# Routing groups and gathered rows spread together over six tiles of 14 up blocks, with one route buffer, a row ring of its own and one of the two one-hots on ScalarE

## The reference

```python
    s1, i1 = lax.top_k(s[:, :, 0], PEER_TOPK)
    s2, i2 = lax.top_k(s[:, :, 1], PEER_TOPK)
    ...
    w = jax.nn.softmax(top_s, axis=-1)
    ...
        a = jnp.einsum('td,thkd->thk', hb, u[ib], preferred_element_type=jnp.float32)
        coef = (wb * jax.nn.gelu(a, approximate=False)).astype(v.dtype)
        return jnp.einsum('thk,thkd->td', coef, v[ib])
```

## Time and profile before

| | us |
|---|---|
| median of 3 runs | 4797.13 |
| lowest, highest | 4784.73, 4804.99 |
| profiled execution, its own time | 4789.41 |
| profiled execution, span of the core | 4787.7 |
| TensorE busy | 4331.5 (90%) |
| VectorE busy | 2986.1 (62%) |
| ScalarE busy | 1384.7 (29%) |
| GpSimd busy | 1407.8 (29%) |
| mean granted TensorE clock | 0.951 of 2.4 GHz |

### The profile page before, as it was taken

How to read it: one execution, slowest core, us unless ns; L and a number is a source line. 1 busy time by engine, 2 the same in 40 slices (tenths; PEclk the granted TensorE clock), 3 DMA queues, 4 the chain that set the end, 5 groups by cost and what they waited for, 6 DMA issues and landing times.

```text
span 4787.7 us, 58551 instructions
## 1 busy us (share of the span) xinstructions
PE 4331.5 (90%) x21163; PEld 3663.4 (77%) x21163; DVE 2986.1 (62%) x3412; ACT 1384.7 (29%) x1485; POOL 1407.8 (29%) x643
## 2 busy tenths in 40 slices
PE   7899998999988998689999998899997899999997
PEld 2587777777766876577999997889986788777776
DVE  1334656445534652554799997677775677777777
ACT  0323232333332121132333444222222233322322
POOL 0002333000001320122566443677761233233330
PEclk9899999999989999889999999899998999999998
DMA  8325665000013664266555568999996899888885
GB/s 287 100 79 156 186 186 160 31 31 26 20 36 114 190 175 113 70 149 149 123 144 143 136 173 204 346 367 360 355 367 244 346 341 345 329 324 333 332 328 182
DMA packets 716549, 967.22 MB, mean 202 GB/s; under 512 B 137467, under 2 KB 535859, under 8 KB 680371
## 3 DMA queue, kind: packets, MB, share of 16 engines
q1 hardware_dynamic: 638531, 613.29, 41.9%
q0 software_dynamic: 40928, 285.23, 15.6%
q10 hardware_dynamic: 37008, 67.65, 4.9%
HBM read 896.84 MB, written 69.22 MB: 202 GB/s over the span
## 4 chain that ended last, share of the span: by engine, by line
PE 45%; DMA 21%; DVE 19%; issue 7%; ACT 4%; SPq 2%; POOL 1%; DVEq 1%; ACTq 0%; POOLq 0%
PE ps L115 14%; PE ps L116 13%; PE ps L117 13%; DMA gel<-gelu_scratch 11%; DMA pu<-in_peer_u_dram 7%; DVE acc L1761 3%; DVE oneJ L1716 3%; DVE vDl L1434 3%; DVE pT L1623 2%; DMA wm<-in_w_mod_dram 2%; PE ps L1881 1%; DVE mred L1314 1%; DVE ring L1738 1%; PE ps L2039 1%; ACT wh L804 1%
## 5 line engine op out<-in xcount | busy, mean ns | idle before, releaser
L728 POOL TENSOR_TENSOR pTul<-pT,pTuh 128x1024 fp32r<-128x1024 f32 x256 | 650.6, 2542 | 500.3 <-ACT pTuh L1082 498.2
L115 PE MATMUL ps<-h2h,pTuh 128*128 128x384 f32 x2048 | 708.4, 346 | 87.0 <-POOL pTul L728 86.0
L115 PE MATMUL ps<-vDh,coh 128*128 128x512 f32 x1536 | 615.1, 400 | 93.9 <-DVE col L1434 93.3
L117 PE MATMUL ps<-h2h,pTul 128*128 128x384 f32 x2048 | 695.5, 340 | 0.0
L116 PE MATMUL ps<-h2l,pTuh 128*128 128x384 f32 x2048 | 695.3, 339 | 0.0
L116 PE MATMUL ps<-vDl,coh 128*128 128x512 f32 x1536 | 609.6, 397 | 0.0
L117 PE MATMUL ps<-vDh,col 128*128 128x512 f32 x1536 | 608.1, 396 | 0.0
L704 POOL TENSOR_TENSOR mbuf<-mbuf,silu 128x2048 f32<-128x2048 f32 x64 | 255.6, 3994 | 1008.8 <-DMA mbuf<-in_w_mod_dram 1008.0
L742 POOL DMA_INDIRECT ring<-in_peer_v_dram,sidx x128 | 325.5, 2543 | 765.2 <-DVE acc L1761 743.3
L1082 ACT ACTIVATE pTuh<-pT 128x1024 fp32r<-128x1024 f32 x256 | 271.9, 1062 | 835.5 <-DVE pT L1623 824.3
L115 PEld LDWEIGHTS ps<-h2h,pTuh 128*128 128x128 f32 x2048 | 393.0, 192 | 98.4 <-POOL pTul L728 84.4
(11 more groups left out here) (328 smaller groups left out, 8046.0 us busy)
## 6 DMA issues: line engine op xcount, KB each, us to landing
vraw<-in_peer_v_dram SPq DMA_DIRECT2D x128, 1024.0 KB
mbuf<-in_w_mod_dram SPq DMA_DIRECT2D x64, 1024.0 KB, 6.0
pu<-in_peer_u_dram ACTq DMA_DIRECT2D x256, 256.0 KB
pu<-in_peer_u_dram SPq DMA_DIRECT2D x256, 256.0 KB
wraw<-in_w_in_dram SPq DMA_DIRECT2D x48, 1024.0 KB, 8.5
wt<-route_scratch SPq DMA_DIRECT2D x128, 384.0 KB
gel<-gelu_scratch SPq DMA_DIRECT2D x128, 384.0 KB
wm<-in_w_mod_dram SPq DMA_DIRECT2D x16, 2048.0 KB, 8.6
```

Source lines behind the costliest of these rows:

```text
L115: pe.matmul(out, lh, rh, start=first, stop=False)
L117: return pe.matmul(out, ll, rh, start=False, stop=last)
L728: pool.tensor_tensor(pTul[s][:, c, :], pT[s][:, c, :], pTuh[s][:, c, :].bitcast(fp32), ALU.subtract).then_inc(u_lo, 1)
```

## The change

The 84 blocks from 40 to 123 are cut into six tiles of 14 blocks (PT, NT). Each tile makes the route table of 64 tokens, 16 groups, and gathers 20 rows of U. TILE_GROUPS and TILE_ROWS tell how many groups and rows each of its blocks carries: groups in blocks 0 to 10 of the tile, one and two in turn, none in the last three. Blocks 124 to 127 carry two rows each.

- There is one route buffer. Its four parts are stored in the last blocks of the tile, parts 1 and 3 by ScalarE in blocks 11 and 12 and parts 0 and 2 by SyncE in blocks 12 and 13; ScalarE waits for them (`r_stored`) in the next tile's first block.
- The ring for U lies at 168, 176, 184 and 192 KB and no longer shares bytes with the route buffer. For V its fourth buffer is at 56 KB (`ring_v`), so GpSimd waits for the last route stores before it gathers V.
- oneJ is made by ScalarE (`one_j`): absd = |second key - iota| with four Abs activations, then Relu(weight - weight x absd) with four Relu activations, which is the weight where the key matches and 0 elsewhere. `nchw` holds the negative weights; VectorE writes it, with one more instruction in each of three top-k rounds. oneI stays on VectorE (`one_i`).
- GpSimd's first gather waits for the last top-k (`tk_chosen`) instead of the route stores. Its loop over blocks 40 to 65 is now written out.
- On SyncE the first loads of V, route table and gelu come after the last up load instead of after block 67's.

```diff
-RI = 4
 GROUPS = TD // 4
-P1 = GROUPS // RI
-LATE = P0 + P1
+PT = 14
+TILE_GROUPS = (1, 2, 1, 2, 1, 2, 1, 2, 1, 2, 1, 0, 0, 0)
+TILE_ROWS = (2, 1, 2, 2, 2, 1, 2, 2, 2, 1, 2, 0, 0, 1)
...
+RT = 64
+NT = TD // RT
+LATE = P0 + NT * PT
...
+        absd = sb("absd", 200, [P, 4, P])
+        nchw = sb("nchw", 94, [P, TD])
         oneJ = [sb(f"oneJ{s}", 40 + 2 * s, [P, 4, P]) for s in range(2)]
         oneI = [sb(f"oneI{s}", 44 + 2 * s, [P, 4, P]) for s in range(2)]
-        RT = 64
-        route = [sb(f"route{s}", (168, 48)[s], [P, NK, RT]) for s in range(2)]
+        route = sb("route", 48, [P, NK, RT])
...
-        ring = [sb(f"ring{k}", (168, 176, 184, 56)[k], [P, D]) for k in range(4)]
+        ring = [sb(f"ring{k}", (168, 176, 184, 192)[k], [P, D]) for k in range(4)]
+        ring_v = ring[0:3] + [sb("ring_v3", 56, [P, D])]
...
-        def rows_before(i):
-            n = max(0, i - LATE - 2)
-            return min(3 * n, 2 * n + 4)
+        def groups_at(i):
+            r, k = divmod(i - P0, PT)
+            g = 16 * r + sum(TILE_GROUPS[:k])
+            return range(g, g + TILE_GROUPS[k]) if P0 <= i < LATE else range(0)
+        def rows_at(i):
+            r, k = divmod(i - P0, PT)
+            if i < P0:
+                return range(0)
+            if i >= LATE:
+                return range(SLOTS - 2 * (NK - i), SLOTS - 2 * (NK - i) + 2)
+            n = sum(TILE_ROWS) * r + sum(TILE_ROWS[:k])
+            return range(n, n + TILE_ROWS[k])
...
+            def route_store(r, k):
+                sp.wait_ge(r_set, 16 * r + 16)
                 i = slice(32 * k, 32 * k + 32)
-                sp.dma_start(route_d[:, i, bass.ds(4 * (n - 16), RT)], route[s][:, i, :]).then_inc(r_stored[s], 16)
+                sp.dma_start(route_d[:, i, bass.ds(RT * r, RT)], route[:, i, :]).then_inc(r_stored, 16)
...
+            with sp.Fori(0, NT) as r:
+                for k in range(PT):
+                    pre_load(PT * r + P0 + k + 2, k % 2)
+                    if k in (12, 13):
+                        route_store(r, 2 * (k - 12))
+                    pre_store(PT * r + P0 + k - 1, (k - 1) % 2)
...
+            for i in range(LATE, NK - 2):
+                pre_load(i + 2, i % 2)
+                pre_store(i - 1, (i - 1) % 2)
+            sp.wait_ge(r_stored, 64 * NT + 16)
+            sp.wait_ge(r_done, GROUPS)
             for s in range(2):
                 sp.wait_ge(g_stored[s], 16 * 2 + 16)
-            sp.wait_ge(r_done, GROUPS)
             v_load(0, 0, 0)
...
-            with pool.Fori(0, LATE // 2 + 1) as i:
+            with pool.Fori(0, P0 // 2) as i:
                 for s in range(2):
                     for h in range(2):
                         u_low(2 * i + s, s, h)
-            pool.wait_ge(tk_chosen, 2)
-            for ss in r_stored:
-                pool.wait_ge(ss, 64 * (TD // RT // 2) + 16)
-            for i in range(LATE + 2, NK):
-                for k in range(rows_before(i), rows_before(i) + 1):
-                    gather_u(k)
+            for i in range(P0, NK):
                 u_low(i, i % 2, 0)
-                for k in range(rows_before(i) + 1, rows_before(i + 1)):
+                if i == P0:
+                    pool.wait_ge(tk_chosen, DB + 2)
+                for k in rows_at(i):
                     gather_u(k)
                 u_low(i, i % 2, 1)
+            pool.wait_ge(r_stored, 64 * NT + 16)
             for k in range(SLOTS):
...
+            def one_j(g, s):
+                if not isinstance(g, int) or g >= 2:
+                    act.wait_ge(r_done, g - 1)
+                if not isinstance(g, int) or g >= 1:
+                    act.wait_ge(oneJ_set, g)
+                for t in range(4):
+                    ins = act.activation(absd[:, t, :], iota[:, :], ACT.Abs, bias=chT[:, 1, bass.ds(4 * g + t, 1)], scale=-1.0)
+                ins.then_inc(oneJ_abs, 1)
+                act.wait_ge(oneJ_abs, g + 1)
+                for t in range(4):
+                    at = bass.ds(4 * g + t, 1)
+                    ins = act.activation(oneJ[s][:, t, :], absd[:, t, :], ACT.Relu, bias=chT[:, 2, at], scale=nchw[:, at])
+                ins.then_inc(oneJ_set, 1)
+            def keep_route(g, q):
                 act.wait_ge(r_done, g + 1)
-                act.activation(route[slot][:, :, 4 * q:4 * q + 4].rearrange("p i t -> p t i"),
-                               pb[k][:, :].rearrange("p (t i) -> p t i", t=4), ACT.Copy).then_inc(r_set, 1)
-            def route_part(r):
-                for k in range(8):
-                    slot, i, s = k // 4, 8 * r + P0 + k, k % 2
-                    if k % 4 == 0:
-                        act.wait_ge(r_stored[slot], 64 * r + 16)
+                act.activation(route[:, :, 4 * q:4 * q + 4].rearrange("p i t -> p t i"),
+                               pb[6 + q % 2][:, :].rearrange("p (t i) -> p t i", t=4), ACT.Copy).then_inc(r_set, 1)
...
+            def route_tile(r):
+                q = 0
+                for k in range(PT):
+                    i, s, n = PT * r + P0 + k, k % 2, TILE_GROUPS[k]
                     pre_hi(i + 1, 1 - s, 1)
                     pre_load(i + 3, 1 - s)
-                    for q in range(RI):
-                        if q == 2:
-                            pre_hi(i + 2, s, 0)
-                        if q == 3:
-                            pre_gelu(i, s)
-                        keep_route(32 * r + 4 * k + q, 6 + q % 2, slot, 4 * (k % 4) + q)
-            with act.Fori(0, TD // RT // 2) as r:
-                route_part(r)
-            with act.Fori(LATE // 2, NK // 2 - 2) as i:
-                for s in range(2):
-                    up_block(2 * i + s, s)
+                    if k in (11, 12):
+                        route_store(r, 2 * (k - 11) + 1)
+                    for w in range(q, q + n):
+                        one_j(16 * r + w, w % 2)
+                    pre_hi(i + 2, s, 0)
+                    if k == 0:
+                        act.wait_ge(r_stored, 64 * r + 16)
+                    if n == 2:
+                        keep_route(16 * r + q, q)
+                    pre_gelu(i, s)
+                    if n:
+                        keep_route(16 * r + q + n - 1, q + n - 1)
+                    q += n
...
-            def one_hots(g, s):
-                if not isinstance(g, int) or g >= 2:
+                dve.tensor_copy(chT[:, :, bass.ts(b, P)], pb[7][:, 0:3 * P].rearrange("p (w t) -> p w t", w=3))
+                dve.tensor_scalar(nchw[:, bass.ts(b, P)], pb[7][:, 2 * P:3 * P], -1.0, None, ALU.mult).then_inc(ch_set, 1)
+            def one_i(g):
+                if g >= 2:
                     dve.wait_ge(r_done, g - 1)
-                for t in range(4):
-                    at = bass.ds(4 * g + t, 1)
-                    dve.tensor_scalar(oneJ[s][:, t, :], iota[:, :], chT[:, 1, at], chT[:, 2, at], ALU.is_equal, ALU.mult)
-                dve.tensor_tensor(oneI[s][:, :, :], iota[:, :].unsqueeze(1).to_broadcast([P, 4, P]),
-                                  chT[:, 0, bass.ds(4 * g, 4)].unsqueeze(2).to_broadcast([P, 4, P]),
-                                  ALU.is_equal).then_inc(one_set, 1)
-            def route_block(i, s, g):
-                one_hots(g, 0)
-                one_hots(g + 1, 1)
-                u_turn(i + 1, 1 - s, 1)
-                one_hots(g + 2, 0)
-                one_hots(g + 3, 1)
-                u_turn(i + 2, s, 0)
-            route_block(P0, 0, 0)
-            route_block(P0 + 1, 1, 4)
-            with dve.Fori(1, P1 // 2) as r:
-                for s in range(2):
-                    route_block(2 * r + P0 + s, s, 8 * r + 4 * s)
+                dve.tensor_tensor(oneI[g % 2][:, :, :], iota[:, :].unsqueeze(1).to_broadcast([P, 4, P]),
+                                  chT[:, 0, 4 * g:4 * g + 4].unsqueeze(2).to_broadcast([P, 4, P]),
+                                  ALU.is_equal).then_inc(oneI_set, 1)
...
-            for i in range(LATE, NK):
+            dve.wait_ge(ch_set, DB)
+            for i in range(P0, NK):
+                groups, rows = groups_at(i), rows_at(i)
+                for g in groups[0:1]:
+                    one_i(g)
                 if i + 1 < NK:
                     u_turn(i + 1, (i + 1) % 2, 1)
-                for k in range(rows_before(i), min(rows_before(i) + 1, rows_before(i + 1))):
+                for k in rows[0:1]:
                     dot(k)
+                for g in groups[1:2]:
+                    one_i(g)
                 if i + 2 < NK:
                     u_turn(i + 2, i % 2, 0)
-                for k in range(rows_before(i) + 1, rows_before(i + 1)):
+                for k in rows[1:2]:
...
+            def route_tile(r):
+                w = 0
+                for k in range(PT):
+                    for q in range(4):
+                        pre_quarter(PT * r + P0 + k, k % 2, q)
+                        if (q == 3 and TILE_GROUPS[k]) or (q == 1 and TILE_GROUPS[k] == 2):
+                            routing(16 * r + w, w % 2)
```

(1 more changed line is left out.)

75 lines of the change are left out of this document (21 added, 54 removed).

## The result

The changed kernel is **slower** by 0.7%: 4826.7 us, the median of 4 runs (4821.4 to 4832.4), against 4795.7 us, the median of 4 runs of the kernel before on the same chip. The ratio is 1.0066 [1.0041, 1.009]: 31 us more, where 57 less were forecast.

What follows compares the result with a forecast made beforehand. Three limits in turn: VectorE, the handover, then DMA with two gathered rows a block. 835 + 27 + 12 + 3 + 3 = 880 us in place of 937, 57 less: 4797.1 - 57 = 4740 us, range 4695 to 4788.

Steps and rivals of the forecast that it cites:

- TensorE's own work, 835 us: Blocks 40 to 127: 88 blocks at 8.4 us of matmuls plus 96 routing groups at 1.0 us.
- absd and oneJ, 0.39 and 0.47 us: ScalarE's Abs and Relu activations, four each a routing group; with overlap and waits 3.0 us a group.
- It waits 0.9 us, in 5 blocks of each of 6 tiles: 27 us: Two-group blocks: ScalarE's first oneJ ready at 5.1 us, wanted by TensorE at 4.2; bounds 0 and 57 us.
- the handover: 2958 to 3060 us before the change: TensorE busy 67.8 of 102 us, clock 0.83; its 21 us were to go.
- so I allow 2 us a tile, 12 us: Tile ends, about blocks 11 and 12: four route stores make two blocks want 9.5 to 10 us of DMA for 8.4.
- The last four blocks, 3 us over today's pace, and 3 us for the V loads: Blocks 124 to 127 keep 9.2 instead of 8.4 us; first V and coefficient loads wait for the last route store.
- VectorE hidden: In a tile VectorE's 92 us hide behind TensorE's 134; a late dot has a block and a half of room.
- everything is hidden: Rival, whole stretch: neither ScalarE nor DMA makes TensorE wait; 99 us less, 4698 us; chance 0.12.
- DMA-bound: Rival, whole stretch: DMA engines bound throughout, 922 us; 15 us less, 4782 us, no change; chance 0.15.
- ScalarE the bound: Rival, tiles: at 4.0 us for a group's oneJ, TensorE loses 57 us, 30 more than forecast; 4770 us; chance 0.08.
- Each tile end costs a handover: Rival, six tile ends: store pieces delay up rows, 18.3 us each; slower, 4838 us; gain gone at 9.5; chance 0.07.

Runs made afterwards that it cites:

- e14: Changed kernel with oneJ one group ahead, tile loops written out, 8 KB route-store pieces, and each tile's two block 0 rows moved to blocks 5 and 9: 4662.6 us.
- e9: e5 with SyncE's gelu stores of blocks 125 and 126 issued ahead of the first and second V load: 4743.1 us.
- e17: e14 with SyncE's last gelu stores issued ahead of the V loads: 4669.4 us.
- e5: Changed kernel with only ScalarE's oneJ made one group ahead, VectorE's oneI left in place: 4748.0 us.
- e12: e9 with the tile loops written out and the route table laid out by tile, so stores go in 8 KB pieces: 4705.8 us.
- e6: Changed kernel with the loops over the tiles written out on TensorE, ScalarE and SyncE: 4786.5 us.

## Why the prediction was wrong

The sum had 880 us for the stretch of 937; the first up matmul of block 40 now starts at 2642.91, the last gelu at 3626.15, so it took 983 (counted from the gelu of block 39, as the blocks below are, 986.6). Against the sum's own parts:

- **TensorE's own work, 835 us: right.** Single-group blocks take 9.3 us, groupless ones 8.4, and e14 takes 832 us from the first matmul of block 40 to the last of block 127.
- **absd and oneJ, 0.39 and 0.47 us: right** (0.388 and 0.480). The 3.0 us for a group was 3.1.
- **"It waits 0.9 us, in 5 blocks of each of 6 tiles: 27 us": the step that failed.** The mechanism was right and the size was not. I started ScalarE's chain as if every part were ready. Outside the loop the wait was 1.45 us and the block 11.8 against 11.3; inside it 1.88 us or more, and in 10 of 20 of these blocks another 1.5 went with the clock. Blocks 3, 5, 7 and 9 of the six tiles were to wait 21.6 us and waited 45 (5.8 in the first tile, 39.3 in the others); block 1 waited longer still. Three things were missing: the split also waits for VectorE, whose oneI I had put at 0.684 us from a mean though the earlier trace rows shows what GpSimd does to its neighbour (1.07 against 3.18); the 0.2 us between chained ScalarE instructions in the loop (1.88 against 1.45 us); and the price of an idle TensorE in clock, which I had read at the handover (0.83) and used only for a rival. Blocks 3, 5, 7 and 9 cost 6.5 us over forecast in the second tile, block 1, where a late up row adds to it, another 4.8. Putting oneJ ahead gave 79 us, more than my 27 to 57: it took away these 45 us of waits, most of the first tile's long one (6.9 us, in its block 1) and the clock lost behind them, and hardly anything of the tile ends (44.7 to 41.3 us of pauses).
- **"so I allow 2 us a tile, 12 us": failed.** By its gelu block 13 alone cost 6.7 us in the second tile, and TensorE's pauses at the ends of the last five tiles come to 44.7 us, 9 a tile. I counted bytes (9.5 to 10 us for 8.4) and not what stands in the queue: the transfer behind a store was held for 12.5 us on both queues. The rows of SyncE's four stores said 15.6 us; I divided it by four. And I put no cost on the two or three gathered rows that follow the stores at once, worth 55 us with the rest mended.
- **The jump at a tile's end had no term at all**, though the diff showed it: a loop body of 14 blocks on ScalarE where there had been 8 and 2. TensorE paused 3.2 to 3.4 us there and ScalarE 3.2 to 4.9, four times. It mattered less than it looks: the loops written out gave 40 us, but not at the tile ends.
- **The last four blocks, 3 us over today's pace, and 3 us for the V loads: failed.** The last four blocks took 46.3 us against 39.6, but e9 and e17 show that it is mostly the down part's wait taken early. What follows the up blocks was 10.4 us shorter.
- **VectorE hidden: right by its busy time (65%)**, wrong in that its lateness passes on. The prediction gave a late dot a block and a half of room; there was none, since ScalarE's chain in the blocks with two groups was already longer than TensorE's two quarters.

The misses of the second tile: 6.5 + 4.8 + 1.3 (block 0) + 6.7 + 0.2 (the rest) - 2 (allowed) = 17.5 us, which is 157.6 against 140.1. Six tiles lose 99, the last blocks 7: 880 + 106 = 986.

The **rivals**: "everything is hidden", 99 us less, is what the tiles can do, though not in this order; e14 is 128 us under the kernel before, 92 of them in this stretch. "DMA-bound" falls: e14 moves 323 GB/s where the changed kernel moved 275. "ScalarE the bound" falls as worded (98 us a tile was about right). "Each tile end costs a handover", at 0.07, named the right place and the right sign: from 9.5 us a tile end the gain is gone. Blocks 13, 0 and 1 cost 10.8 of the 17.5 us over forecast. It needed no 18 us hole, because the groups took the other half of the gain. I gave it too little since I priced each part by its average and never added the small ones.

The rule of the Trainium skill, ScalarE: Activation LUTs, Rules for kernel authors (such operations belong on VectorE), would have been right for this kernel, 4773 against 4827 us, and wrong for the mended one, 4745 against 4717.5: the place in the order weighed more than the engine.

## What to carry to other kernels

Where engines run in a written-out order, a mean load of two thirds says nothing: take the tightest block, start the chain with what it really waits for, and ask whether the work can be made one step ahead; that alone turned 31 us lost into 44 won. When several stalls stand behind each other, mending one moves it to the next block: long pieces gave 6 us alone and 39 with oneJ ahead, moved rows 28 alone and 55 on top of the rest, so a single edit that gives nothing does not clear its cause. A wait that the profile lays to one engine belongs to another where that one's last instruction ended long before.

## What was not expected of the hardware

- A short pause of TensorE may or may not be followed by a lower granted clock. In the changed kernel 6 of 16 pauses of 1.88 or 1.89 us were followed by 0.50 (1.2 GHz) for 2 us and more, the other 10 by 1.00 (the one that ends at 2863.96), as were the four of 1.45 us. A longer one decides it no better: one of 3.32 us in e5, which ends at 3205.32, was followed by 1.00 too.
- Behind two stores of 4096 pieces of 256 bytes each the next transfer was held 12.0 us (ScalarE) and 12.8 us (SyncE). Behind two with 8 KB pieces it took 0.89 and 0.36 us (e12, from 3202 us on).
- At the jump of a loop of 14 blocks ScalarE paused 3.2 to 4.9 us and TensorE 3.2 to 3.4 us, and in the loop oneJ waited some 0.2 us each time for the absd ahead of it (14.7 us in 76), which it did not with the loop written out (e6).
- oneI, one TENSOR_TENSOR of 128x512, takes between 0.644 and 2.026 us, its median 1.988, in the changed kernel:

```profile
L1722 DVE TENSOR_TENSOR oneI<-iota,chT x96: 644/1988/2026, 2643.0 to 3534.5; 128x512 f32<-128x512 f32 x96
```

It had a mean of 0.684 while four TENSOR_SCALARs stood ahead of it and met GpSimd's subtraction in its place.
